# A two-block transformer kernel: expert up weights in two-row runs, expert rows turned by every second column, and a gather that leaves out empty slots

## The chip, the cores and the metric

One core of a Trainium2 chip runs the whole kernel. The metric is the device time of one launch in microseconds. All arithmetic is on float32 data. One profiled execution stands beside the timed runs. PE is the matrix engine (TensorE), PEld its weight loads, DVE, ACT and POOL are the vector, scalar and GpSimd engines, and SPq is the queue of the sync engine, which issues most DMAs.

## The reference, cut to what matters

The program is two transformer blocks over 512 tokens of 1024 features. Nearly all of it (the state-space, mLSTM and gated-linear-attention mixers, two convolutional feed-forward layers, sparse attention, memory attention) is the same before and after. The change is in the last part, a mixture of 32 experts of which each token takes two:

```
def hier_moe(h, w_rg, b_rg, w_re, b_re, w_up, w_down):
    g_logits = (h @ w_rg + b_rg)                      # 4 groups, one is taken
    e_logits = (h @ w_re + b_re)                      # 8 experts in a group, two are taken
    ...
    for n in range(N_EXPERTS):                        # 32
        a, b = jnp.split(h @ w_up[n], 2, axis=-1)     # w_up[n]: 1024 x 512
        out = out + combine[:, n:n + 1] * ((jax.nn.silu(a) * b) @ w_down[n])   # w_down[n]: 256 x 1024
    return out
```

`combine` is zero for every expert that a token did not take, so the kernel computes only the pairs of token and expert that count: 2 x 512 = 1024 of them.

## The kernel before

The expert part runs in four stages, each a block of instruction streams that all engines enter and leave together.

**Route** (line 3678) computes the two experts of each token on DVE. Meanwhile SP stores the normalised rows to a DRAM tensor (`normalised_rows`) and loads the weights of experts 0 and 1 ahead of need (`first_experts`, line 4258).

**Place** (line 3796) gives every pair of token and expert a slot. A block is 96 slots (`ROWS`) of one expert. Every expert has one block of its own, and there are ten more for experts with over 96 tokens (`NB` is 42). The result is `r.token`, the token number of each slot of each block, built by a product of 0/1 matrices on PE. A slot that nobody fills gets 0 from it, so the gather reads row 0 of the table for it. SP meanwhile writes zeros to the result rows of the ten further blocks. POOL has nothing to do in this stage.

**Experts** (line 3917) goes over the blocks. In the trace there are 32 of them, one per expert: 32 up loads, 32 down loads, 32 stores and 32 gathers. For block n the steps are:

- SP loads `up` (1024 x 512, 2 MB, into the buffer `ring`) and `down` (256 x 1024, 1 MB, into `moe_down`). Both have two sides, so a load goes to the side of the block two before. The up load of block n + 2 waits until the up products of block n are done (`up_done`). The down load of n + 1 waits until the down weights of n - 1 are split (`down_split`).
- POOL copies the 96 token numbers of the block and issues an indirect DMA (line 4010) that gathers 96 rows of 4 KB into one side of `e.rows` (`expert_rows`). It waits until the rows of block n - 2 have been turned.
- PE turns the gathered rows (`turn_rows`, line 4024): eight transposes of 96 x 128, each of them one weight load of the rows and one matmul against the identity. DVE copies the result to `e.x`.
- PE multiplies (`first`, line 4035): 32 products of a 128 x 128 piece of `up` with 96 columns of `e.x`, each two passes, so 64 matmuls in the trace.
- ACT and DVE apply silu and the gate, and split the hidden values and the down weights into a high and a low part (lines 4071 to 4139).
- PE multiplies by `down` (`second`, lines 384 to 386): 12 matmuls of 512 columns.
- ACT copies the result out of the accumulator and SP stores 96 rows to DRAM.

Each engine has a software pipeline written by hand: in step n, PE does `first(n + 1)`, then `turn_rows(n + 2)`, then `second(n)`. Two steps stand ahead of a loop, the loop takes two blocks a turn, and two steps stand behind it. SP's order in a step is down load of n + 1, up load of n + 2, store of n - 1.

The up weights are read by rows d = t * 128 + p, where p is the SBUF partition and t one of eight pieces. One partition so gets eight rows that lie 128 rows apart, as eight runs of 2 KB.

**Combine** (line 4158) gathers for each token its two result rows (eight indirect DMAs from POOL), scales and adds them on DVE, and stores the output.

Of the kernel before, what the change touches and what calls it, by code (L numbers as in the profile page):

```python
# [22 lines left out]
ALU = mybir.AluOpType  # L23
# [3 lines left out]
P = 128  # L27
T = 512
NT = T // P
# [37 lines left out]
NE, EPG, NG, EF = 32, 8, 4, 256  # L67
# [3722 lines left out]
ROWS = 96  # L3790
MOST = -(-T // ROWS)
NB = 2 * -(-(NE + SLOTS // ROWS) // 2)
FTE = EF // P


def place(k, r, zeros, y_dram, y_zeroed):

    nc = k.nc  # L3800
    with nc.Block(no_gpsimd_drain=True) as block:
        @block.sync
        def _(sp):
            sp.wait_ge(*k.sa(1))
            sp.dma_start(y_dram[NE * ROWS:, :].rearrange("(s p) d -> p s d", p=ROWS),
                         zeros[0:ROWS, :].rearrange("p (o d) -> p o d", o=1).to_broadcast([ROWS, NB - NE, D])).then_inc(y_zeroed, 16)
# [21 lines left out]
        def _(dve):  # L3828
            nc.vector.memset(zeros[:, :], 0.0).then_inc(k.sa.sem, 1)
            ps = k.ps[:, 0, :]  # L3830
# [43 lines left out]
            dve.drain()  # L3874
            nc.vector.tensor_copy(r.row[:, :], r.row_f[:, :])
            for t in range(NT):
                nc.vector.tensor_scalar(r.token_id[:, t:t + 1], ps[:, (NT + 1) * NE:(NT + 1) * NE + 1], float(t * P - 1), None, ALU.add)
            dve.drain()
            for n in range(2 * NT):
                nc.vector.tensor_scalar(r.is_slot[:, n, :], r.iota[:, 0:ROWS], r.rank[:, n:n + 1], None, ALU.is_equal)  # L3880
# [19 lines left out]
            nc.vector.tensor_scalar(r.before_last[:, :], r.count[:, :], -1.0, None, ALU.add)  # L3900
            nc.vector.tensor_scalar(r.expert[:, :], r.expert_f[:, :, 0], float(NE - 1), None, ALU.min)
            dve.wait_ge(*k.pb(1))
            nc.vector.tensor_copy(r.token[0:ROWS, :], k.ps[0:ROWS, 1, 0:NB])
    k.pa.close(1)
    k.va.close(1)
    k.pb.close(1)
# [3 lines left out]
def at_block(n, times=1, more=0):  # L3910

    if isinstance(n, tuple):
        return n[0] * (2 * times) + (n[1] * times + more)
    return n * times + more


def experts(k, r, rows_dram, y_dram, up, dn, e):
# [1 line left out]


    nc, A = k.nc, k.A
    wu = A["w_up_2"][0].rearrange("e (t p) n -> e p t n", p=P)
    wd = A["w_down_2"][0].rearrange("e (t p) n -> e p t n", p=P)

    XB, UB, YB = 0, 2, 4

    def side(n):
        return n[1] % 2 if isinstance(n, tuple) else n % 2

    def early(n, before):  # L3930

        return not isinstance(n, tuple) and n < before
# [5 lines left out]
    def pair_before_last(queue):  # L3938
        return queue.value_load(r.before_last[0:1, 0:1], min_val=0, max_val=NB // 2 - 2)
# [13 lines left out]
    def later(n, d):  # L3953

        return (n[0], n[1] + d, n[2]) if isinstance(n, tuple) else n + d

    def inside(n, d):

        return n[1] + d < n[2] if isinstance(n, tuple) else n + d >= 0

    with nc.Block(no_gpsimd_drain=True) as block:
        @block.sync
        def _(sp):
            def expert_of(n):
                at = at_block(n)
                one = r.expert[0:1, bass.ds(at, 1)] if isinstance(n, tuple) else r.expert[0:1, at:at + 1]
                return nc.sync.value_load(one, min_val=0, max_val=NE - 1)

            def load_up(n, expert):
                sp.dma_start(up[side(n)], wu[bass.ds(expert, 1)].rearrange("o p t n -> p (o t) n")).then_inc(e.up_loaded[side(n)], 16)  # L3970

            def load_down(n, expert):
                sp.dma_start(dn[side(n)], wd[bass.ds(expert, 1)].rearrange("o p t n -> p (o t) n")).then_inc(e.down_loaded[side(n)], 16)

            def of_last_pair(n):
                return isinstance(n, tuple) and n[1] >= 2 and n[2] == 4

            def store(n):
                sp.wait_ge(e.y_ready, at_block(n, 1, 1))
                sp.dma_start(y_dram[bass.ds(at_block(n, ROWS), ROWS), :] if isinstance(n, tuple) else y_dram[n * ROWS:(n + 1) * ROWS, :],  # L3980
                             e.y[0:ROWS, side(n), :]).then_inc(e.y_ended if of_last_pair(n) else e.y_stored[side(n)], 16)

            def step(n):
                if inside(n, -1) and inside(n, 1):
                    expert = expert_of(later(n, 1))
                    sp.wait_ge(e.down_split, at_block(n))
                    load_down(later(n, 1), expert)
                if inside(n, 2):
                    expert = expert_of(later(n, 2))
                    sp.wait_ge(e.up_done, at_block(n, 1, 1))  # L3990
                    load_up(later(n, 2), expert)
                if inside(n, -1):
                    store(later(n, -1))

            before = pair_before_last(nc.sync)
            sp.wait_ge(e.y_zeroed, 16)
            each_block(sp, before, step)
            store((before, 3, 4))

            sp.wait_ge(e.y_ended, 32)  # L4000

        @block.gpsimd
        def _(pool):
            def step(n):
                s = side(n)
                if not early(n, 2):
                    pool.wait_ge(e.turned, at_block(n, 1, -1))
                nc.gpsimd.tensor_copy(e.slot_token[0:ROWS, s:s + 1], r.token[0:ROWS, bass.ds(at_block(n), 1)] if isinstance(n, tuple) else r.token[0:ROWS, n:n + 1])
                pool.drain()
                nc.gpsimd.indirect_dma_start(e.rows[0:ROWS, s, :], None, rows_dram, bass.IndirectOffsetOnAxis(ap=e.slot_token[0:ROWS, s:s + 1], axis=0))\  # L4010
                    .then_inc(e.gathered[s], 16)

            each_block(pool, pair_before_last(nc.gpsimd), step)
            pool.drain()

        @block.tensor
        def _(pe):
            def turn_rows(n):
                s = side(n)
                pe.wait_ge(e.gathered[s], pair(n, 16))  # L4020
                if not early(n, 1):
                    pe.wait_ge(e.x_ready, at_block(n))
                for c in range(KD):
                    last = nc.tensor.transpose(k.ps[:, XB + c // NT, (c % NT) * ROWS:(c % NT + 1) * ROWS], e.rows[0:ROWS, s, c * P:(c + 1) * P], k.ident[0:ROWS, 0:ROWS])
                last.then_inc(e.turned, 1)

            def first(n):
# [177 lines left out]
def moe(k, out):  # L4205

    nc, A, sb = k.nc, k.A, k.alloc
    with ExitStack() as c:
        wr = router_place(k)
        r = Kernel()  # L4210
# [25 lines left out]
        e = Kernel()  # L4236
# [16 lines left out]
        up = [k.ring[:, s, :].rearrange("p (t n) -> p t n", t=KD) for s in range(2)]  # L4253
        dn = [down[:, s, :, :] for s in range(2)]
        rows_dram = nc.dram_tensor("normalised_rows", (T, D), F32, kind="Internal").ap()
        y_dram = nc.dram_tensor("expert_results", (NB * ROWS, D), F32, kind="Internal").ap()

        def first_experts(sp):
            for n in range(2):
                sp.dma_start(up[n], A["w_up_2"][0][n].rearrange("(t p) n -> p t n", p=P)).then_inc(e.up_loaded[n], 16)  # L4260
                sp.dma_start(dn[n], A["w_down_2"][0][n].rearrange("(t p) n -> p t n", p=P)).then_inc(e.down_loaded[n], 16)
        route(k, wr, r, k.ytmp[:, :, :], rows_dram, first_experts)
        place(k, r, e.zeros, y_dram, e.y_zeroed)
        experts(k, r, rows_dram, y_dram, up, dn, e)
        picked = k.ring[:, :, :].rearrange("p s n -> p (s n)").rearrange("p (n d) -> p n d", n=2 * NT)
        combine(k, r, y_dram, picked, out)
# [43 lines left out]
```

## Time and profile before

| | us |
|---|---|
| Median of 3 runs | 2733.13 |
| Lowest, highest | 2729.95, 2734.3 |
| Span of the profiled execution | 2731.6 |
| Mean granted TensorE clock | 0.973 |
| PE, PEld busy | 2544.9 (93%), 2032.0 (74%) |
| DVE, ACT, POOL busy | 1481.8 (54%), 1020.1 (37%), 226.4 (8%) |
| DMA | 329.04 MB, mean 120 GB/s |

The profiled execution's own time is its span, 2731.6 us from first to last instruction; the median of the runs is 1.5 us above that. The expert part is the last fifth: route begins at 2301 us, place at 2322, experts at 2345, combine at 2708. Shares of busy time over the whole span say little about it. The views have to be read for its own stretch, with the timeline of one block as the unit, since all 32 blocks do the same. A matmul's end in the trace is modelled, so the distance from one start to the next tells what it takes, and not its duration.

### The profile page before, as it was taken

To read this page: it belongs to the slowest core of one execution; us is meant where nothing else is said; L and a number is where in the kernel's file an instruction comes from. 1 tells how busy PE (TensorE), PEld (TensorE's weight loads), DVE (VectorE), ACT (ScalarE), POOL (GpSimd) and SP (SyncE) were. 2 spreads that over 40 slices of the span, in tenths; PEclk is the share of its full clock that TensorE was granted. 3 is DMA by queue.
4 is the path that set the end of the run, shared out by engine and by line. 5 is a ranking of instruction groups with operands and counts; after the bars stand their busy time and mean duration, and the time that the engine had idled before them with its cause. 6 is when DMAs were issued, how large, how long until landed. Compare 5 with 4: busy or idle time off the path is not lost. (4 is left out here: it accounts for less than half of the span.)

```text
span 2731.6 us, 34315 instructions
## 1 busy us (share of the span) xinstructions
PE 2544.9 (93%) x12689; PEld 2032.0 (74%) x12689; DVE 1481.8 (54%) x2251; ACT 1020.1 (37%) x1706; POOL 226.4 (8%) x260
## 2 busy tenths in 40 slices
PE   6999997789999999999999999999898988799995
PEld 5777786667888885766788887687586767699994
DVE  5766445654555534744555544477897564433333
ACT  3423342334544425423444433433334522133331
POOL 0000001000000000000000000555141000111111
PEclk9999999999999999999999999999999998799997
DMA  4122231032333321112333422222021013699995
GB/s 144 70 85 93 93 108 51 28 139 77 92 92 96 137 93 63 62 62 78 93 92 100 127 96 93 95 82 93 32 86 38 31 71 108 226 372 375 371 375 200
DMA packets 212513, 329.04 MB, mean 120 GB/s; under 512 B 13873, under 2 KB 110033, under 8 KB 212401
## 3 DMA queue, kind: packets, MB, share of 16 engines
q1 hardware_dynamic: 206784, 310.43, 33.1%
q0 software_dynamic: 4736, 16.78, 2.0%
q8 instruction: 70, 1.15, 0.2%
q10 hardware_dynamic: 881, 0.34, 0.0%
q14 instruction: 42, 0.34, 0.0%
HBM read 298.43 MB, written 29.10 MB: 120 GB/s over the span
## 5 line engine op out<-in xcount | busy, mean ns | idle before, releaser
L384 PE MATMUL ps<-ffn_parts 128*128 128x512 f32 x1056 | 411.6, 390 | 2.5 <-DVE ffn_parts L379 1.7
L386 PE MATMUL ps<-ffn_parts 128*128 128x512 f32 x1056 | 410.9, 389 | 0.0
L385 PE MATMUL ps<-ffn_parts 128*128 128x512 f32 x1056 | 410.8, 389 | 0.0
L4035 PEld LDWEIGHTS ps<-expert_x,ring 128*128 128x128 f32 x2048 | 235.0, 193 | 8.1 <-DVE expert_x L4119 3.3
L4035 PE MATMUL ps<-expert_x,ring 128*128 128x96 f32 x2048 | 234.9, 276 | 3.8 <-DVE expert_x L4119 3.0
L384 PEld LDWEIGHTS ps<-ffn_parts 128*128 128x128 f32 x1056 | 198.2, 188 | 46.5 <-issue 2.6
L386 PEld LDWEIGHTS ps<-ffn_parts 128*128 128x128 f32 x1056 | 198.2, 188 | 41.4
L385 PEld LDWEIGHTS ps<-ffn_parts 128*128 128x128 f32 x1056 | 198.2, 188 | 40.8
L379 DVE TENSOR_TENSOR ffn_parts<-ring,ffn_parts 128x1024 fp32r<-128x1024 f32 x132 | 157.7, 1223 | 117.9 <-ACT ffn_parts L2334 107.4
L379 POOL TENSOR_TENSOR w_lo<-ring,w_hi 128x512 fp32r<-128x512 f32 (+1 forms) x112 | 160.0, 1433 | 720.9 <-ACT w_hi L543 720.6
L2385 DVE SCALAR_TENSOR_TENSOR y_tmp<-ps,pcol,y_tmp 128x511 f32<-128x511 f32 x88 | 61.9, 745 | 214.0 <-ACT y_tmp L2318 214.0
L379 DVE TENSOR_TENSOR front_w_lo<-ring,front_w_hi 128x512 fp32r<-128x512 f32 x104 | 71.5, 688 | 138.6 <-ACT front_w_hi L925 138.4
L925 ACT CAST front_w_hi<-ring 128x512 fp32r<-128x512 f32 x104 | 63.9, 618 | 219.8 <-PE ps L386 219.7
L301 PE MATMUL ps<-brow,ident 128*128 128x512 f32 x238 | 119.1, 641 | 22.6 <-PEq L1827 6.1
L543 ACT CAST w_hi<-ring 128x512 fp32r<-128x512 f32 (+1 forms) x112 | 68.2, 610 | 185.4 <-PE ps L386 178.0
L379 DVE TENSOR_TENSOR expert_down_lo<-moe_down,expert_down_hi 128x1024 fp32r<-128x1024 f32 x64 | 75.5, 1222 | 96.4 <-ACT expert_down_hi L4079 96.4
L3331 DVE SCALAR_TENSOR_TENSOR conv_gate<-conv_u,pcol,conv_gate 128x512 f32<-128x512 f32 x120 | 114.2, 999 | 1.8
L384 PE MATMUL ps<-kept_hi,w_hi 128*128 128x512 f32 x256 | 101.5, 396 | 3.7 <-POOL w_lo L379 2.5
L2318 ACT ACTIVATE y_tmp<-ps,pcol 128x512 f32<-128x512 f32 x88 | 63.7, 774 | 109.7 <-PE ps L386 109.5
L384 PE MATMUL ps<-front_h_hi,front_w_hi 128*128 128x512 f32 (+1 forms) x232 | 97.5, 420 | 4.4 <-ACT hst L1256 2.7
L301 PEld LDWEIGHTS ps<-brow,ident 128*128 128x128 f32 x238 | 46.2, 205 | 74.5 <-issue 73.9
L384 PE MATMUL ps<-wo_hi,lhs_hi 128*128 128x512 f32 x256 | 100.5, 393 | 0.4 <-DVE lhs_lo L379 0.4
(636 smaller groups left out, 5210.1 us busy)
## 6 DMA issues: line engine op xcount, KB each, us to landing
ring<-in_w_up SPq DMA_DIRECT2D x32, 2048.0 KB, 11.4
ring<-in_ffn_w_up SPq DMA_DIRECT2D x88, 512.0 KB, 4.9
moe_down<-in_w_down SPq DMA_DIRECT2D x32, 1024.0 KB
ring<-in_ab_w_in SPq DMA_DIRECT2D x13, 2048.0 KB, 7.7
ring<-in_w_in SPq DMA_DIRECT2D x11, 2048.0 KB, 7.9
ring<-in_ffn_w_down SPq DMA_DIRECT2D x10, 2048.0 KB, 7.7
ring<-in_c_w_in SPq DMA_DIRECT2D x6, 2048.0 KB, 8.0
expert_results<-expert_y SPq DMA_DIRECT2D x32, 384.0 KB, 7.7
```

The source lines that it names most:

```text
L301: k.nc.tensor.matmul(k.ps[:, bank, :], k.ident[:, :], k.brow[:, 0:BANK], start=True, stop=True)
L379: return engine.tensor_tensor(lo, whole, hi.bitcast(F32), ALU.subtract)
L384: nc.tensor.matmul(out, left[0], right[0], start=start, stop=False, **more)
L385: nc.tensor.matmul(out, left[0], right[1], start=False, stop=False, **more)
L386: return nc.tensor.matmul(out, left[1], right[0], start=False, stop=stop, **more)
L543: nc.scalar.copy(part(w_hi, p), chunk(j)[:, rows, cols]).then_inc(k.w_hi_ready.sem, 1)
L925: k.nc.scalar.copy(self.part(0, p), self.raw(p)).then_inc(k.w_hi_ready.sem, 1)
L2318: last = nc.scalar.activation(ybuf[:, s, half, :], bank(s, half), ACT.Identity, bias=column(bias, i, s, half), scale=column(tap1, i, s, half))
L2385: nc.vector.scalar_tensor_tensor(out=ybuf[:, s, half, 1:T], in0=bank(s, half)[:, 0:T - 1], scalar=column(tap0, i, s, half), in1=ybuf[:, s, ...
L3331: nc.vector.scalar_tensor_tensor(out=y[:, j, :], in0=u[:, j, i:i + T], scalar=tap[:, n:n + 1], in1=y[:, j, :], op0=ALU.mult, op1=ALU.add)
L4035: last = nc.tensor.matmul(k.ps[:, UB + s, m * ROWS:(m + 1) * ROWS], up[s][:, c, m * P:(m + 1) * P], e.x[:, s, c, :], start=(c == 0), stop= ...
```

## The change

Four edits that belong together:

- `up_rows` and `up_runs` read and write the up weights so that a partition gets rows d = t * 256 + 2 * p and the one after it as one run of 4 KB, with t one of four pieces. The buffer, its size and the way `first` reads it stay: piece c now holds the rows t * 256 + 2 * p + b with t = c // 2 and b = c % 2.
- `turn_rows` has to turn the same features for piece c. It takes every second column of a stretch of 256 columns, beginning with column c % 2, where it took 128 columns in a row. There are still eight transposes of 96 x 128.
- `place` makes an unfilled slot's token number 1024 (2 * T) in place of 0: it subtracts 2 * T ahead of the product and adds it behind. The gather has a bounds check at row 511, and a number beyond it is skipped without an error.
- Rows that are skipped keep what was in the buffer. So that this is never uninitialised, `place` now clears `e.rows` on POOL (128 x 2048 values).

What is multiplied for filled slots is the same; what stands in unfilled slots is not read by combine.

```
+def up_rows(w):
+    return w.rearrange("e (t p b) n -> e p t (b n)", p=P, b=2)
+def up_runs(ap):
+    return ap.rearrange("p (t b) n -> p t (b n)", b=2)
...
-def place(k, r, zeros, y_dram, y_zeroed):
+def place(k, r, zeros, rows, y_dram, y_zeroed):
...
+        @block.gpsimd
+        def _(pool):
+            nc.gpsimd.memset(rows, 0.0)
+            pool.drain()
...
-                nc.vector.tensor_scalar(r.token_id[:, t:t + 1], ps[:, (NT + 1) * NE:(NT + 1) * NE + 1], float(t * P - 1), None, ALU.add)
+                nc.vector.tensor_scalar(r.token_id[:, t:t + 1], ps[:, (NT + 1) * NE:(NT + 1) * NE + 1], float(t * P - 1 - 2 * T), None, ALU.add)
...
-            nc.vector.tensor_copy(r.token[0:ROWS, :], k.ps[0:ROWS, 1, 0:NB])
+            nc.vector.tensor_scalar(r.token[0:ROWS, :], k.ps[0:ROWS, 1, 0:NB], float(2 * T), None, ALU.add)
...
-    wu = A["w_up_2"][0].rearrange("e (t p) n -> e p t n", p=P)
+    wu = up_rows(A["w_up_2"][0])
...
-                sp.dma_start(up[side(n)], wu[bass.ds(expert, 1)].rearrange("o p t n -> p (o t) n")).then_inc(e.up_loaded[side(n)], 16)
+                sp.dma_start(up_runs(up[side(n)]), wu[bass.ds(expert, 1)].rearrange("o p t n -> p (o t) n")).then_inc(e.up_loaded[side(n)], 16)
...
-                nc.gpsimd.indirect_dma_start(e.rows[0:ROWS, s, :], None, rows_dram, bass.IndirectOffsetOnAxis(ap=e.slot_token[0:ROWS, s:s + 1], axis=0))\
+                nc.gpsimd.indirect_dma_start(e.rows[0:ROWS, s, :], None, rows_dram, bass.IndirectOffsetOnAxis(ap=e.slot_token[0:ROWS, s:s + 1], axis=0), bounds_check=T - 1, oob_is_err=False)\
                     .then_inc(e.gathered[s], 16)
...
-                    last = nc.tensor.transpose(k.ps[:, XB + c // NT, (c % NT) * ROWS:(c % NT + 1) * ROWS], e.rows[0:ROWS, s, c * P:(c + 1) * P], k.ident[0:ROWS, 0:ROWS])
+                    features = e.rows[0:ROWS, s, (c // 2) * 2 * P:(c // 2 + 1) * 2 * P].rearrange("r (p b) -> r b p", b=2)[:, c % 2, :]
+                    last = nc.tensor.transpose(k.ps[:, XB + c // NT, (c % NT) * ROWS:(c % NT + 1) * ROWS], features, k.ident[0:ROWS, 0:ROWS])
...
-                sp.dma_start(up[n], A["w_up_2"][0][n].rearrange("(t p) n -> p t n", p=P)).then_inc(e.up_loaded[n], 16)
+                sp.dma_start(up_runs(up[n]), up_rows(A["w_up_2"][0])[n]).then_inc(e.up_loaded[n], 16)
```

PE, ACT, DVE and SP issue their instructions in the same order and number as before. On POOL one instruction comes in. From the end of route to the first two gathers its queue was, before:

```order
61 L3689 UNCONDITIONAL_BRANCH
62 L4002 UNCONDITIONAL_BRANCH
63 L3939 TENSOR_LOAD moe_before_last
64 L3939 ISA x2
65 L4008 COPY expert_slot_token<-moe_token 96x1
66 L4010 DMA expert_rows<-normalised_rows,expert_slot_token 96x1024
```

and it is, in the changed kernel (line 3954 there is line 3939 before, 4023 is 4008, 4025 is 4010):

```order
61 L3689 UNCONDITIONAL_BRANCH
62 L3812 UNCONDITIONAL_BRANCH
63 L3814 MEMSET expert_rows 128x2048
64 L3811 UNCONDITIONAL_BRANCH
65 L4017 UNCONDITIONAL_BRANCH
66 L3954 TENSOR_LOAD moe_before_last
67 L3954 ISA x2
68 L4023 COPY expert_slot_token<-moe_token 96x1
69 L4025 DMA expert_rows<-normalised_rows,expert_slot_token 96x1024
```

The memset stands in the place stage, where POOL had no instruction; everything behind it is in the old order.

## Rows read from the trace of the kernel before

**Rows 1.** The page: 40 slices of 68.3 us, busy tenths of PE, and GB/s
```profile
PE   6999997789999999999999999999898988799995
...
GB/s 144 70 85 93 93 108 51 28 139 77 92 92 96 137 93 63 62 62 78 93 92 100 127 96 93 95 82 93 32 86 38 31 71 108 226 372 375 371 375 200
```

**Rows 2.** Busy us of each engine by stretch; then clock, DMA share, GB/s
```profile
core 0: us, PE busy (x) PEld busy (x) DVE busy (x) ACT busy (x) POOL busy (x), PEclk, DMA share, GB/s
2400.00:2650.00 250.00, 250.00 (x1986) 230.29 (x1986) 94.89 (x144) 84.41 (x140) 26.81 (x48) 1.00 1.03 373
```

**Rows 3.** Timeline, weight loads, one block: start us, us, engine, line, operation, count
```profile
2480.80 7.34 PEld L4035 LDWEIGHTS ps<-expert_x,ring 128*128 128x128 f32 x64
2488.04 0.75 PEld L4024 LDWEIGHTS ps<-ident,expert_rows 96*128 96x128 f32 x8
2488.73 0.16 PEld L384 LDWEIGHTS ps<-expert_down_hi,expert_hid_hi 128*96 128x96 f32 x1
...
2491.37 7.34 PEld L4035 LDWEIGHTS ps<-expert_x,ring 128*128 128x128 f32 x64
...
2501.94 7.34 PEld L4035 LDWEIGHTS ps<-expert_x,ring 128*128 128x128 f32 x64
```

**Rows 4.** Waits of the matmul engine, 2345 to 2710 us: us in total, times, longest
```profile
PE ps L384 <- DVE expert_down_lo L379: 4.6, 1, 4.6
PE ps L4035 <- DVE expert_x L4119: 3.0, 2, 1.9
...
PE ps L4024 <- DMA expert_rows<-normalised_rows,expert_slot_token: 0.6, 1, 0.6
```

**Rows 5.** Line 3970, the up load, on the SP queue: 30 issues and their landing
```profile
L3970 SPq DMA_DIRECT2D ring<-in_w_up x30: 372/373/397, 2360.7 to 2668.1; - x30
...
DMA to landing us min/median/max: 9.0/11.3/12.7
```

**Rows 6.** Timeline of the SP queue in the block of Rows 3
```profile
2485.89 0.38 SPq L3973 DMA_DIRECT2D moe_down<-in_w_down  x1
2488.49 0.37 SPq L3970 DMA_DIRECT2D ring<-in_w_up  x1
```

**Rows 7.** The page's DMA queues, and loads by kind: KB each, us to landing
```profile
q0 software_dynamic: 4736, 16.78, 2.0%
...
ring<-in_ab_w_in SPq DMA_DIRECT2D x13, 2048.0 KB, 7.7
...
ring<-in_ffn_w_down SPq DMA_DIRECT2D x10, 2048.0 KB, 7.7
```

**Rows 8.** DMA view of 2296 to 2350 us, slices of 1.35 us
```profile
GB/s 0 0 0 0 231 370 400 352 206 231 338 370 364 422 423 402 401 394 388 411 428 382 346 334 282 291 337 325 285 240 106 55 30 0 0 0 0 0 0 249
```

**Rows 9.** Timeline of the matmul engine at the start of the expert stage
```profile
2345.18 5.46 PE L301 MATMUL ps<-brow,ident 128*128 128x512 f32 x6 [0.61 <-PEq L3801]
2351.18 0.88 PE L4024 MATMUL ps<-ident,expert_rows 96*128 96x96 f32 x8 [0.55 <-DMA expert_rows<-normalised_rows,expert_slot_token]
...
2353.18 7.22 PEld L4035 LDWEIGHTS ps<-expert_x,ring 128*128 128x128 f32 x64 [1.30 <-DVE expert_x L4119]
```

**Rows 10.** Windows of the same place, columns as in Rows 2
```profile
2346.00:2350.00 4.00, 4.00 (x6) 1.33 (x4) 0.00 (x0) 2.42 (x3) 1.47 (x3) 0.50 0.24 84
2350.00:2354.00 4.00, 2.33 (x16) 1.52 (x16) 1.90 (x3) 0.00 (x0) 1.13 (x2) 0.85 0.15 31
```

**Rows 11.** Line 4010, the gather: duration ns least, median, greatest; landing
```profile
L4010 POOL DMA_INDIRECT expert_rows<-normalised_rows,expert_slot_token x32: 937/938/1128, 2347.1 to 2659.2; - x32
...
DMA to landing us min/median/max: 3.9/7.5/8.7
```

**Rows 12.** Line 2566, a POOL memset of 128 by 2048
```profile
L2566 POOL MEMSET gla_att<- x1: 1806/1806/1806, 1126.4 to 1126.4; 128x2048 f32 x1
```

**Rows 13.** Timeline of DVE in the placement stage
```profile
2323.57 0.23 DVE L3835 TENSOR_SCALAR moe_iota<-moe_iota 128x128 f32<-128x128 f32 x1
2328.63 0.19 DVE L3838 TENSOR_SCALAR moe_blocks<-ps 128x32 f32<-128x32 f32 x1 [4.83 <-PE ps L3819]
```

More of the change, by code:

```diff
@@ L4259, in first_experts @@
             for n in range(2):
-                sp.dma_start(up[n], A["w_up_2"][0][n].rearrange("(t p) n -> p t n", p=P)).then_inc(e.up_loaded[n], 16)
+                sp.dma_start(up_runs(up[n]), up_rows(A["w_up_2"][0])[n]).then_inc(e.up_loaded[n], 16)
                 sp.dma_start(dn[n], A["w_down_2"][0][n].rearrange("(t p) n -> p t n", p=P)).then_inc(e.down_loaded[n], 16)
         route(k, wr, r, k.ytmp[:, :, :], rows_dram, first_experts)
-        place(k, r, e.zeros, y_dram, e.y_zeroed)
+        place(k, r, e.zeros, e.rows[:, :, :], y_dram, e.y_zeroed)
         experts(k, r, rows_dram, y_dram, up, dn, e)
```

## Prediction

> **What bounds the kernel now.** I began with the page's 40 slices [rows 1]: the traffic jumps from about 100 to 371-375 GB/s in slices 36 to 39, the expert stage, and nowhere else. That invites the reading "bound by DMA", and the change cuts traffic and packets there. But the same slices show PE at 9, so I asked the table by stretch [rows 2]: from 2400 to 2650 us PE is busy 250.00 of 250.00 us and PEld 230.29, with DMA at a share of 1.03 and 373 GB/s. Both look full, so busy shares don't decide it. What does is who waits for whom.
>
> The timeline of one block [rows 3]: 64 up passes start at 2480.80, the eight transposes at 2488.04, the 12 down products at 2488.73, the next up passes at 2491.37. So a block is 7.24 + 0.69 + 2.64 = 10.57 us, and the next one (2501.94) again 10.57. In the whole expert stage the waits of PE are few [rows 4]: 4.6 us at the end for the last down weights, which are split only behind the last copies, 3.0 us in two waits for the first columns, and 0.6 us for the first gather. None is for a weight load, and the first two are for DVE's work, not for bytes.
>
> Is PE itself slowed by the traffic? The first block's 64 up passes, with DMA at a share of 0.15 to 0.31, took 7.22 us [rows 9, 10]; under full traffic the same 64 take 7.24 from first start to the transposes. So no. And DMA keeps ahead: the up load of block n + 2 is issued at 2488.49 [rows 6] and is needed when the up passes after next begin, 2501.94 [rows 3], 13.45 us later. It lands after 11.3 us as a median and 12.7 at most [rows 5]. The least reserve is 13.45 - 12.7 = 0.75 us. It is thin, but it is there 30 times of 30. The loop is paced by PE. The DMA is busy because each block asks for 2048 + 1024 + 384 + 384 KB = 3.93 MB, and 3.93 MB / 10.57 us = 372 GB/s is the demand, not a ceiling: in the burst of route's stores and loads the queues moved up to 428 GB/s [rows 8].
>
> **The change part by part.** The sum is made against the span of 2731.6; the median of the runs lies 1.5 above it.
>
> (a) Up loads in 4 KB runs: 512 packets of 4 KB for 1024 of 2 KB. Two kinds of 2 MB load in this trace differ in just that: columns of `ab_w_in` come in 2 KB runs, rows of `ffn_w_down` in 4 KB runs, and both land after 7.7 us [rows 7]. So for a lone load I put the gain at 0. Among other transfers it may be above 0 or slightly below; either way it changes the reserve of 0.75 us, not the 10.57. It counts only if a load became over 6% slower (0.75 / 12.7), which the equal 7.7 excludes. 0 us.
>
> (b) Gather without empty slots: 32 x 96 = 3072 rows become 1024, so 2048 x 4 KB = 8.4 MB less, 0.26 MB a block, 6.7% of its 3.93 MB. In steady state a gather is issued just behind the turning of block n - 2 and used two periods later; it lands after 7.5 us, at most 8.7 [rows 11], of about 20. Cover: PE's own 21.1 us of work. 0 us. Exposed is the first gather alone: PE stands 0.55 us for it [rows 9]. If fewer rows land sooner, 0 to 0.55 us are won, beyond which the three filling products (to 2350.64) end last. If the check makes the descriptors' computation longer, it is lost; the nearest row is the least landing of a gather, 3.9 us, and one that took twice as long would cost 3.9. I take a gain of 0.3, since fewer rows mean fewer packets and the check is one comparison per row; ends -0.55 and +3.9.
>
> (c) The transposes read every second column. This is the one edit on the pacing engine: 8 x 32 = 256 weight loads, eight of them from 2488.04 to 2488.73, 86 ns each [rows 3]. No weight load of the trace has a stride of two. Bounds: no cost, since the 128 columns and 96 rows are the same; upward, reading at half the pace. A 128-column piece at the pace of the 512-column products (12 in 2.64 us, so 220 ns for 512 columns, 0.43 ns a column) is 55 ns, and twice that adds 55 ns x 256 = 14.1 us; all of a transpose doubled, 0.69 x 32 = 22.1 us. Below nothing is excluded: nothing is read less. I take 0, as the nearest row is the transpose itself, with the same columns, rows and count. This is a choice, not a reading, and the largest risk.
>
> On this the Trainium skill, Advanced Engine Details and Errata, section SBUF Cachelines, says that SBUF is read in lines of 16 bytes and that two hits on a line are enough for full pace. Four float32 values lie in a line, and every second one is two hits, so by that page the cost is 0; no row here shows it. Were the page wrong here, the sum would be the 14.1 us above.
>
> (d) The memset of 128 x 2048 on POOL: the trace has one of that very size, 1.81 us [rows 12]. It runs in place, where POOL has nothing else from 2322 to 2345. Even if it held up DVE's first instructions, DVE then idles 4.83 us for PE [rows 13], which covers 1.81; should the cover go, the cost is 1.81 at most. 0 us.
>
> (e) The two changed DVE instructions (another constant; an add for a copy, 96 x 42) are one for one: 0 us. PE's, SP's and ACT's instructions keep number and order.
>
> (f) The loads ahead in route: the traffic is at 0 by 2342 [rows 8], and the first up passes start at 2353.18. 0 us. The tail behind 2682 waits for ACT and DVE, and combine's eight gathers are untouched. 0 us.
>
> Sum: -0.3 us. 2731.6 - 0.3 = 2731.3, and with the 1.5 to the median 2732.8.
>
> **The rivals.**
>
> *Every second column costs (slower).* If a weight load at stride two is read at half pace, PE's block grows from 10.57 by 8 x 55 ns = 0.44 us and the whole by 14.1: 2733.1 + 14.1 = 2747.2. It speaks for it that PE has no gap to hide a nanosecond in; against it, that a transpose of 128 columns stands at 86 ns from the next where 128 columns at the pace of (c) are 55, so part of a slower load could lie in what is there already. From 5.5 us / 256 = 21 ns per transpose on it would show. Chance 0.10.
>
> *DMA sets the pace after all (faster).* If the 373 GB/s were the ceiling and PE only happened to look full (its ends are modelled), the block would shrink with its bytes: 0.26 MB / 373 GB/s = 0.70 us a block, over 31 blocks 21.8 us: 2711.3. For: DMA share 1.03, reserve 0.75 us. Against: no wait of PE for a load [rows 4], equal pace in light traffic [rows 9, 10], 428 GB/s seen [rows 8]. Chance 0.05.
>
> The Trainium skill speaks for this rival: DMA: Bandwidth & Descriptors, section "Where 436 GB/s comes from", has the HBM side bind at about 358 GB/s for a core. By that rule 373 would be past the ceiling and the stage bound by it. The trace disagrees: 373 is held for 250 us and 400 to 428 in a burst.
>
> *The checked gather is slow at the start (slower).* If the first gather takes twice its 3.9 us, PE stands 3.9 more, and its clock, 0.50 from 2346 to 2350 and 0.85 in the next four [rows 10], rises as much later; up to 4 us of work at half pace cost 2 more. 2733.1 + 5.9 = 2739.0. Chance 0.04. Later gathers have 21.1 - 8.7 = 12.4 us of reserve and don't matter.
>
> *The change doesn't do what it says.* Skipped rows may be moved anyway, or the packets stay at 2 KB. Then nothing is won, and by (a) and (b) nothing was to be won, so the time is as forecast. It lies within that case and is told apart by counts alone.
>
> **How the numbers follow.** A measurement of this kernel can tell about 0.2%, 5.5 us, from no change. Forecast within it: 0.80, at 2732.8. Faster: the DMA rival's 0.05 and 0.01 for something unseen, 0.06. Slower: 0.10 + 0.04 = 0.14. Same: 0.80. The range for 8 in 10: downward 0.55 for the gather, 3.2 for the spread of the runs (2733.13 to 2729.95) and two more for the median of other runs, 2727; upward it takes in the slow first gather, 2739.0, and 1 us for the spread, 2740. The cases at 2747 and 2711 stay out, 0.15 together, and 0.05 of the rest.
>
> **What would show it.** Right: the block still 10.57 us; PE 250.00 of 250.00 in mid-stage; the eight transposes still 0.69; GB/s in slices 36 to 39 down from 373 to about 348 (3.67 MB / 10.57); the software queue at 4736 - 2048 = 2688 packets and 8.4 MB, from the 4736 and 16.78 MB of before [rows 7]; up loads landing sooner than 11.3; the first wait of PE for the gather gone. Wrong: transposes longer than 0.69 (stride); a shorter distance between up passes (DMA or something in the passes); first transposes of the stage later than 2351.2 (gather); DVE's instruction at 2328.6 later (memset).

## The result, and the profile after

| | us |
|---|---|
| Changed kernel, median of 12 runs | 2739.59 (2735.72 to 2746.19) |
| Kernel before, median of 12 runs beside them | 2730.56 (2725.44 to 2738.81) |
| Ratio, 95% interval | 1.0033 (1.0021 to 1.0045) |
| Span of the profiled execution | 2737.8 |

The change costs 0.33%, 9.0 us of 2730.56. I had forecast 2732.8 and no change; 2739.59 lies just inside my range, but the sign was wrong: it is slower beyond its interval. That it lies inside is luck, as the part on the prediction says.

First the table by stretch for mid-stage, as [rows 2] has it of before, and the stage's start, as [rows 10]. The columns are busy us of PE, PEld, DVE, ACT and POOL, then granted clock, DMA share, GB/s.

```profile
2346.00:2350.00 4.00, 2.20 (x13) 1.94 (x13) 1.98 (x3) 0.00 (x0) 1.18 (x2) 0.89 0.10 22
2350.00:2354.00 4.00, 4.00 (x21) 4.00 (x21) 1.31 (x2) 0.00 (x0) 0.98 (x1) 0.50 0.11 28
2400.00:2650.00 250.00, 250.00 (x1940) 231.13 (x1940) 92.86 (x140) 83.74 (x138) 26.69 (x46) 1.00 0.93 338
```

PE is full in mid-stage, before and after. But in 250 us it gets 1940 matmuls done where it did 1986. DMA went from a share of 1.03 to 0.93, and 373 to 338 GB/s. So the traffic fell as meant, and the engine that it was not meant for became slower. The timeline of the weight loads shows where, against [rows 3]:

```profile
2482.98 7.35 PEld L4051 LDWEIGHTS ps<-expert_x,ring 128*128 128x128 f32 x64
2490.22 1.05 PEld L4040 LDWEIGHTS ps<-ident,expert_rows 96*128 96x128 f32 x8
2491.16 0.20 PEld L384 LDWEIGHTS ps<-expert_down_hi,expert_hid_hi 128*96 128x96 f32 x1
...
2493.82 7.35 PEld L4051 LDWEIGHTS ps<-expert_x,ring 128*128 128x128 f32 x64
```

The 64 up passes take 7.24 us, as before. The eight transposes take 0.94 for 0.69, the 12 down products 2.66 for 2.64. A block is 10.84 us for 10.57: 0.27 us more, 31 times over 8.4 us. The answer by line shows the weight load of a single transpose (least, median, greatest duration in ns), before and now:

```profile
L4024 PEld LDWEIGHTS ps<-ident,expert_rows x256: 138/140/171, 2351.2 to 2678.8; 96*128 96x128 f32 x128
...
L4040 PEld LDWEIGHTS ps<-ident,expert_rows x256: 195/216/218, 2346.8 to 2686.2; 96*128 96x128 f32 x128
```

A load is 76 ns longer. Loads overlap with their neighbours (140 ns long, 86 ns apart before), so what a transpose costs more is the distance from one start to the next: 0.25 / 8 = 31 ns.

The counts. The page's totals of before and of after, one from each:

```profile
DMA packets 212513, 329.04 MB, mean 120 GB/s; under 512 B 13873, under 2 KB 110033, under 8 KB 212401
```

```profile
DMA packets 196129, 320.66 MB, mean 117 GB/s; under 512 B 15921, under 2 KB 112081, under 8 KB 196017
q0 software_dynamic: 4736, 8.40, 1.0%
...
ring<-in_w_up SPq DMA_DIRECT2D x32, 2048.0 KB, 10.3
```

There are 16,384 packets fewer (32 loads times 512) and 8.38 MB less. The software queue has 8.40 MB for 16.78, but its 4736 packets are all there: 2048 more are under 512 B. A skipped row still sends a packet, with nothing in it. Up loads land after 10.3 us (11.4 on the page of before). The waits of PE in the stage are those of [rows 4] (the columns: line, what it waited for, us in total, times, longest):

```profile
PE ps L384 <- DVE expert_down_lo L379: 4.6, 1, 4.6
PE ps L4051 <- DVE expert_x L4135: 2.7, 2, 1.6
PE ps L4040 <- DMA expert_rows<-normalised_rows,expert_slot_token: 0.7, 1, 0.7
```

**The account of the profiled execution.** Its span grew by 6.2 us, which is not 8.4, so other things moved. The timeline at the start of the stage, against [rows 9]:

```profile
2340.93 5.18 PE L301 MATMUL ps<-brow,ident 128*128 128x512 f32 x6 [0.61 <-PEq L3811]
2346.79 1.20 PE L4040 MATMUL ps<-ident,expert_rows 96*128 96x96 f32 x8 [0.68 <-DMA expert_rows<-normalised_rows,expert_slot_token]
2349.10 10.47 PEld L4051 LDWEIGHTS ps<-expert_x,ring 128*128 128x128 f32 x64 [1.28 <-DVE expert_x L4135]
```

The stage began at 2340.93 for 2345.18, 4.25 us earlier. Of the change only the first two loads, the memset and two DVE instructions lie ahead of it, and neither part alone gives a gain in the medians below, so I don't count it as won. From there to the first gather of combine (2708.42 before, 2714.46 now) it took 373.53 us for 363.24, 10.29 more. By pieces between starts of up passes: 0.17 to the first; 3.52 from the first to the third, of which 3.25 is the first block's 64 passes alone, 10.47 us for 7.22; 7.71 from the third to the last; and 1.11 less behind the last. The sum is 10.29. The 3.25 is the clock, but not because it rose late. Asked by single microseconds, it rose here between 2345 and 2346, stood at 1.00 from 2346 to 2349, and was back at 0.50 from 2350 to 2355, under the first up passes (the 0.89 and 0.50 above). Before, it rose between 2351 and 2352 and stayed at 1.00 until 2364, so that the first block ran whole at 2.4 GHz. What PE did ahead of it is alike in both traces: six matmuls, a wait for the gather, eight transposes, a wait of 1.1 us for the columns. The 1.11 is the clock too: the last six down products, which started 0.43 us apart before, started 0.23 to 0.29 us apart now. Only the 7.71 is the block's 0.27. Whether the 3.25 belongs to the change is asked of the runs below.

### The profile page after: what moved, and what is told of

Read it like the earlier page. It is cut to its first block and busy times, and to the rows that moved or that the text cites. A ratio compares the mean times of both kernels' runs of the same rounds, so it can differ in the third digit from the quotient of the medians.

```text
span 2737.8 us, 34349 instructions
## 1 busy us (share of the span) xinstructions
PE 2552.6 (93%) x12689; PEld 2040.2 (75%) x12689; DVE 1482.0 (54%) x2251; ACT 1020.1 (37%) x1706; POOL 229.3 (8%) x261
## 2 busy tenths in 40 slices
DMA packets 196129, 320.66 MB, mean 117 GB/s; under 512 B 15921, under 2 KB 112081, under 8 KB 196017
## 3 DMA queue, kind: packets, MB, share of 16 engines
q0 software_dynamic: 4736, 8.40, 1.0%
## 6 DMA issues: line engine op xcount, KB each, us to landing
ring<-in_w_up SPq DMA_DIRECT2D x32, 2048.0 KB, 10.3
```

## The experiments

All ratios are against runs of the kernel before on the same chip. The first four divide the change into its parts.

### Only the columns

```
-  transpose(..., e.rows[0:ROWS, s, c * P:(c + 1) * P], ...)
+  features = e.rows[0:ROWS, s, (c // 2) * 2 * P:(c // 2 + 1) * 2 * P].rearrange("r (p b) -> r b p", b=2)[:, c % 2, :]
+  transpose(..., features, ...)
```

> The kernel before with one edit: the eight transposes of a block take every second column. Up weights stay in 2 KB runs, all 96 rows are gathered. Features and weight rows are paired wrongly, the work is the same. Theory (the weight load at stride two costs): the block grows from 10.57 to 10.84 us as in the changed kernel, the transposes from 0.69 to 0.94 and the step to the down products by 0.02, so 31 x 0.27 = 8.4 us, ratio about 1.0031. Rival (the loss comes with the gather's check or the first blocks' clock): ratio 1.000, block 10.57.

Measured: 2740.83 us for 2730.38; ratio 1.0033 (1.0022 to 1.0044). The timeline of one block, weight loads:

```profile
2475.65 7.35 PEld L4036 LDWEIGHTS ps<-expert_x,ring 128*128 128x128 f32 x64
2482.89 1.05 PEld L4025 LDWEIGHTS ps<-ident,expert_rows 96*128 96x128 f32 x8
...
2486.49 7.35 PEld L4036 LDWEIGHTS ps<-expert_x,ring 128*128 128x128 f32 x64
```

The block is 10.84 us. This one line alone gives the whole ratio of the change, with the traffic of before.

### Only the 4 KB runs

```
-  wu = A["w_up_2"][0].rearrange("e (t p) n -> e p t n", p=P)
+  wu = up_rows(A["w_up_2"][0])
-  sp.dma_start(up[side(n)], ...
+  sp.dma_start(up_runs(up[side(n)]), ...
```

> The kernel before with one edit: up weights in 4 KB runs. Transposes in plain columns, so features and weight rows are paired wrongly; the work is the same. Theory: block 10.57, ratio 1.000 +- 0.001; up loads land sooner than 11.3 us or equal, and nobody waits for them. Rival (fewer packets free the DMA and it sets the pace in part): ratio below 0.998.

Measured: 2730.36 us; 1.0002 (0.9992 to 1.0013). The block is 10.57 us (2474.07 to the next at 2484.63), the up loads land after 11.4 us as before, with 196129 packets for 212513. The edit is worth nothing here.

### Only the skipped rows

```
-  float(t * P - 1)             +  float(t * P - 1 - 2 * T)
-  tensor_copy(r.token, ...)    +  tensor_scalar(r.token, ..., float(2 * T), None, ALU.add)
+  nc.gpsimd.memset(rows, 0.0)
-  indirect_dma_start(...)      +  indirect_dma_start(..., bounds_check=T - 1, oob_is_err=False)
```

> The kernel before with one edit: empty slots skipped by the bounds check, with the memset. Computes the reference. Theory: block 10.57, ratio 1.000 +- 0.001, 338 GB/s in mid-stage, software queue 8.4 MB and still 4736 packets. Rival (the checked gather costs at the start and leaves the clock low in the first block, 10.47 us for its 64 passes against 7.22): ratio 1.0015, first up passes over 10 us.

Measured: 2729.64 us; 0.9993 (0.9983 to 1.0003). Its mid-stage traffic and the stage's first up passes:

```profile
2400.00:2650.00 250.00, 250.00 (x1986) 230.25 (x1986) 93.81 (x142) 85.28 (x142) 27.89 (x48) 1.00 0.99 347
```

```profile
2348.65 10.47 PEld L4040 LDWEIGHTS ps<-expert_x,ring 128*128 128x128 f32 x64 [1.30 <-DVE expert_x L4124]
2359.02 0.75 PEld L4029 LDWEIGHTS ps<-ident,expert_rows 96*128 96x128 f32 x8
```

PE does the same 1986 matmuls in 250 us, on 347 GB/s in place of 373 (the 338 that I had expected belongs to the longer block of the whole change). The edit is free and worth nothing. This kernel also has the 10.47 us in its first block, with plain transposes and a median that is not above that of before. So the 3.25 us can't be put down to the stride, and the medians show no such cost for the skipped rows: the same 64 passes took 7.22 us in the trace of before, 8.85 in those of the 4 KB runs and of the ordered rows (next), 10.39 with only the columns. One trace's start of the stage can be off by 3 us for the clock alone. That the stride makes the long first block likelier isn't excluded, since all three traces with strided transposes have it (every fourth column, below, too) and of five with the plain up and transpose loads only this one. The runs speak against it: the mean granted clock is 0.9749 over the 12 of the changed kernel and 0.9745 over the 32 of the kernel before.

### The whole change, rows put in order by ACT

The transposes are plain again. The columns are put in the order that the up weights now want when the rows go to DRAM, once for 512 rows:

```
-  transpose(..., features, ...)
+  transpose(..., e.rows[0:ROWS, s, c * P:(c + 1) * P], ...)
+  for t in range(NT):
+      nc.scalar.copy(ordered[:, t, :].rearrange("p (q b c) -> p q b c", b=2, c=P), rows[:, t, :].rearrange("p (q c b) -> p q b c", b=2, c=P))
+  sp.wait_ge(rows_ordered, 1)
-  sp.dma_start(rows_dram..., rows)     +  sp.dma_start(rows_dram..., ordered)
```

> The changed kernel, but the transposes take 128 columns in a row again. The order that the 4 KB runs need is made once, by ACT: in route it copies the four tiles of normalised rows (every second column first) into a buffer of its own, and SP stores that one for the gathers. Computes the reference. Theory: the stride moves from PE's 256 weight loads to four ACT copies of about 1.04 us that nobody waits for; block 10.57, ratio to before 1.000 +- 0.001. Rival: a stage behind the later store or the later prefetch starts late, ratio up to 1.0016 (4.5 us).

Measured: 2733.05 us; 1.0007 (0.9996 to 1.0018). A block, and the four copies on ACT:

```profile
2472.29 7.34 PEld L4054 LDWEIGHTS ps<-expert_x,ring 128*128 128x128 f32 x64
2479.53 0.75 PEld L4043 LDWEIGHTS ps<-ident,expert_rows 96*128 96x128 f32 x8
...
2482.86 7.34 PEld L4054 LDWEIGHTS ps<-expert_x,ring 128*128 128x128 f32 x64
```

```profile
2306.07 4.18 ACT L3775 COPY rows_ordered_sb<-y_tmp 128x1024 f32<-128x1024 f32 x4 [1.28 <-PEq L620]
```

The block is 10.57 again. Both DMA edits are in, all of the loss is out, and there is no gain. It is the better form of the change, not a better kernel than before. Whether the stride is free for ACT isn't settled by this: its four copies are 1.12 us long each and start 1.02 us apart, where its plain casts of a tile of that size (line 2313 before) are 1.05 us long and, two in a row, start 0.94 us apart. But a cast is another operation, and the difference is 0.08 us a copy at most, four times in all.

### Does the price grow with the stride?

My theory behind the first runs was that the load reads lines of SBUF and pays for the ones it touches: every fourth column touches twice as many as every second. The rival was a fixed price for a load that is not plain. Runs of four rows (8 KB) need every fourth column:

```
-  "e (t p b) n -> e p t (b n)", p=P, b=2    +  ... b=4
-  (c // 2) * 2 * P ... b=2)[:, c % 2, :]    +  (c // 4) * 4 * P ... b=4)[:, c % 4, :]
```

> The changed kernel with runs of four rows (8 KB) and transposes of every fourth column. Computes the reference. Theory (the price goes with the lines of 16 bytes that a weight load touches: 32 for 128 plain columns, 64 at stride two, 128 at stride four): going from stride one to two cost 32 ns a transpose, so two to four costs about 64 to 110 more, the block 11.3 to 11.7 us, ratio to before 1.008 to 1.013. Rival (any stride costs the same fixed 32 ns): block 10.84, ratio 1.0033. The Trainium skill, Advanced Engine Details and Errata, section SBUF Cachelines, has two hits on a line free and one hit slow: the measured stride two was not free.

Measured: 2741.01 us for 2729.78; 1.0033 (1.0021 to 1.0045). The answer by line, weight loads of the transposes:

```profile
L4040 PEld LDWEIGHTS ps<-ident,expert_rows x256: 197/219/222, 2348.9 to 2688.3; 96*128 96x128 f32 x128
```

The block is 10.84 again, the load 219 ns for 216. My theory asked for 11.3 to 11.7 and falls: stride four costs what stride two does.

### Every second value of the other operand

```
-  e.x[:, s, c, :]
+  e.x[:, s, c // 2 * 2:c // 2 * 2 + 2, :].rearrange("p a m -> p (a m)").rearrange("p (m b) -> p b m", b=2)[:, c % 2, :]
```

> The kernel before; the 64 up passes of a block read their moving operand (96 columns of expert_x) at every second column, the weights plain. Pairs features wrongly, the work is the same. Theory (a matmul's 96 columns hide beside the next weight load of 128, so a slower read of them has some cover): block 10.57 to 10.7, ratio below 1.002. Rival (the moving side pays 32 / 128 x 96 = 24 ns a pass uncovered): block longer by 1.5 us, ratio 1.018.

Measured: 2732.07 us; 1.0001 (0.9989 to 1.0012), block 10.56 us (up passes at 2454.21 and 2464.76). As the moving operand of all 2048 up passes, every second value is free. So the price belongs to the weights.

### What a pass waits for: columns or weights

The up passes multiply 64 of the 96 slots; the last 32 slots of each block are left out:

```
-  k.ps[:, UB + s, m * ROWS:(m + 1) * ROWS], ..., e.x[:, s, c, :]
+  k.ps[:, UB + s, m * ROWS:m * ROWS + 64],  ..., e.x[:, s, c, 0:64]
```

> The kernel before; the 64 up passes of a block multiply 64 columns in place of 96, the last 32 slots of a block are left out there. It asks how much of the 7.24 us goes with columns and how much with the 128-column weight loads, and whether PE time saved comes back as time. Theory: passes go from 113 to about 100 ns (route's passes of 36 columns were 182 ns apart at half clock, 91 at full), 0.8 us a block on PE, of which the DMA, paced at about 10 us a block in the half kernels, gives back only 0.6: ratio 0.993. Rival (weight loads alone set a pass): ratio 1.000.

Measured: 2746.39 us; 1.0053 (1.0034 to 1.0072), with a third fewer columns. Two places of its timeline:

```profile
2355.41 13.73 PEld L4035 LDWEIGHTS ps<-expert_x,ring 128*128 128x128 f32 x64 [1.30 <-DVE expert_x L4119]
2368.91 1.40 PEld L4024 LDWEIGHTS ps<-ident,expert_rows 96*128 96x128 f32 x8
2371.85 13.73 PEld L4035 LDWEIGHTS ps<-expert_x,ring 128*128 128x128 f32 x64 [1.54 <-DVE expert_x L4119]
...
2453.79 7.35 PEld L4035 LDWEIGHTS ps<-expert_x,ring 128*128 128x128 f32 x64
2461.00 0.75 PEld L4024 LDWEIGHTS ps<-ident,expert_rows 96*128 96x128 f32 x8
2464.32 7.35 PEld L4035 LDWEIGHTS ps<-expert_x,ring 128*128 128x128 f32 x64
```

In mid-stage a block is 10.53 us for 10.57, so a pass stays at 113 ns (7.21 / 64) with 64 columns for 96. It is paced by its weight load of 128 by 128, not by its columns, and my 100 ns was wrong. I had taken it from route's passes of 36 columns (line 3710), which I read as 91 ns apart at the full clock. They are 64 passes in 11.67 us with the clock falling among them: the first stand 112 ns apart at 1.00 and the others 213 at 0.50. The trace of before thus had the answer.

The loss is at the two ends of the stage. The traced run took 2754.45 us, the slowest of the five. In it the first two blocks ran whole at 1.2 GHz (granted clock 0.50 from 2356 to 2380) and took 35.18 us from the first up passes to the third, where before they took 21.96: 13.2 us. From the last up passes to the first gather of combine it took 32.0 us for 25.6, again at 0.50 for most of it. The low clock is not that one run's: the mean granted clock of the five is 0.965 to 0.970, of the 20 runs of before beside them 0.971 to 0.977. What PE did that delayed its clock is not settled.

### A strided load in an ordinary pass

The weights of the up products, every second hidden column, so that the hidden values come out in another order:

```
-  up[s][:, c, m * P:(m + 1) * P]
+  up[s][:, c, m // 2 * 2 * P:(m // 2 + 1) * 2 * P].rearrange("p (n b) -> p b n", b=2)[:, m % 2, :]
```

> The kernel before; the 64 up passes of a block load their 128 columns of weights at every second column (of 256), transposes plain. It permutes the hidden columns, the work is the same. Theory (a plain transpose loads its weights in a faster way, 86 ns apart, and a stride takes it back to about the pace of an ordinary float32 pass, 113 ns; so an ordinary pass has nothing to lose): block 10.57 to 10.8, ratio 1.000 to 1.002. Rival (any 128-column load at a stride pays 31 ns): block longer by 64 x 31 ns = 2.0 us, 62 us in all, ratio 1.023.

Measured: 2744.81 us for 2730.63; 1.0055 (1.0033 to 1.0077). Weight loads of a block:

```profile
2450.65 7.73 PEld L4035 LDWEIGHTS ps<-expert_x,ring 128*128 128x128 f32 x64
2458.27 0.76 PEld L4024 LDWEIGHTS ps<-ident,expert_rows 96*128 96x128 f32 x8
...
2461.60 7.73 PEld L4035 LDWEIGHTS ps<-expert_x,ring 128*128 128x128 f32 x64
```

The 64 passes take 7.62 us, 119 ns each, for 113. A block is 10.95 us for 10.57, which over 31 blocks is 11.8 us, a ratio of 1.0043. That lies inside the interval and above the 1.002 that my theory allowed, so an ordinary pass does have something to lose, if far less than the rival's 31 ns. A strided transpose takes 0.94 / 8 = 118 ns by the group, and 119 from one start to the next inside it. So both kinds end at the same 119 ns. A plain up pass stands at 113 ns and loses 6; a plain transpose stands at 86 ns and loses 32. That is what my terms had wrong: I asked how fast columns stream, and the question was how fast the load is, which is not the same for the two kinds.

Why a plain transpose stands at 86 can be read further in the trace of before, where other stages transpose too (weight loads by line; the last numbers before the waits are us busy and mean ns of one):

```profile
L4035 PEld LDWEIGHTS ps<-expert_x,ring 128*128 128x128 f32 x2048 | 235.0, 193 | 8.1 <-DVE expert_x L4119 3.3 <-issue 1.3
L662 PEld LDWEIGHTS ps<-ident,y_tmp 128*128 128x128 f32 x64 | 7.0, 140 | 6.1 <-DVE y_tmp L738 5.7
```

The transposes of line 662 have 128 rows and 128 moving columns. Their load is as long as that of the experts' transposes, 140 ns, but they stand 7.0 / 64 = 109 ns apart. With 96 columns it is 86. So a plain transpose goes with its columns (0.85 and 0.90 ns a column) and its load, shorter than the 193 ns of an ordinary pass, hides beside them, while the ordinary pass and every strided one go with the load. From this an estimate: a stride in a transpose of 128 columns would cost 119 - 109 = 10 ns, not 32. No run tried it, and the two kinds of transpose differ in their rows as well.

### What the DMA edits are worth when PE is out of the way

Half of the up products are left out (`for c in range(0, KD, 2)`), in four kernels: of before, with the 4 KB runs, with the skipped rows, and with both (rows ordered as above). PE then needs 10.57 less 3.62, 6.95 us a block.

> The kernel before with half of the up products left out (every second piece c), so that PE needs 3.62 + 0.69 + 2.64 = 6.95 us a block and no longer sets the pace; loads, gathers and stores are all there. Theory: the 3.93 MB a block now take at least 3.93 / 428 = 9.2 us, so the block lands at 9.2 to 9.8 us and PE waits for up loads. If the DMA had been the pace before too, the block would stay at 10.57 and the time at ratio 1.000.

> As h1_half_before, with the up weights in 4 KB runs. Where DMA sets the pace this tells what fewer packets are worth. Theory (packets cost little, since lone loads of both kinds land after 7.7 us): block as in h1_half_before to 0.1 us. Rival (a packet costs a fixed time): block shorter by up to 0.5 us, 15 us in all.

> As h1_half_before, with the empty slots skipped. Theory: 6.7% fewer bytes, block shorter by 0.26 MB / 400 GB/s = 0.6 us, 20 us in all (ratio to h1_half_before about 0.993).

> As h1_half_before, with 4 KB runs, skipped slots and the rows put in order by ACT in route, so without the stride on PE. Theory: the sum of the two before it, block about 0.6 to 0.8 us shorter than h1_half_before, nothing lost to the stride.

| up products halved | median us | ratio to before (interval) | us a block, issues | us a block, mid-stage |
|---|---|---|---|---|
| nothing else | 2714.40 | 0.9934 (0.9915 to 0.9954) | 10.24 | 10.34 |
| 4 KB runs | 2709.62 | 0.9910 (0.9893 to 0.9926) | 10.04 | 10.17 |
| skipped rows | 2700.07 | 0.9880 (0.9863 to 0.9897) | 9.78 | 9.92 |
| both | 2698.98 | 0.9874 (0.9857 to 0.9890) | 9.60 | 9.72 |

The fourth column is from the first to the last of the 30 up issues, over 29. It takes in the first blocks, whose loads were done ahead; for the kernel before it is 10.60. The last column is from the fifth up passes to the thirtieth (2386.16 and 2644.70 in the first kernel), over 25, and it is the one to hold against 10.57. Three answers of the first kernel: by stretch, PE's waits from 2380 to 2620 us, and the up loads:

```profile
2400.00:2600.00 200.00, 152.65 (x1011) 129.69 (x1010) 78.39 (x119) 69.85 (x117) 22.34 (x40) 0.94 1.04 378
```

```profile
PE ps L4035 <- issue: 31.7, 12, 3.5
PE ps L4035 <- DMA ring<-in_w_up: 24.0, 11, 3.2
```

```profile
L3970 SPq DMA_DIRECT2D ring<-in_w_up x30: 372/373/397, 2354.9 to 2651.9; - x30
...
DMA to landing us min/median/max: 11.2/15.6/17.0
```

Taking 3.62 us of PE's work out of every block gave back 0.23 in mid-stage; I had expected 9.2 to 9.8 us a block. PE now stands before its up passes once a block, 23 times in 240 us. For 11 of these waits (24.0 us) the trace names the up load, for 12 (31.7 us) it names nothing. The load lands after 15.6 us where it took 11.3 [rows 5]. A block's 3.93 MB in 10.34 us are 380 GB/s, and the table has 378 at a DMA share of 1.04. So the DMA sets the pace here, and in the kernel before it was 0.23 us a block from doing so, no more. How much of this is the rate of the transfers and how much that a load waits for its buffer, these runs don't separate.

In this setting the skipped rows are worth 14.3 us (2714.40 to 2700.07), with intervals that do not touch, and 0.42 us a block, where I had expected 0.6. The 4 KB runs are worth 4.8 us with intervals that overlap, and both together are not measurably better than the skipped rows alone. The traces lean towards a small gain of the 4 KB runs: 0.17 us a block without and 0.20 with the skipped rows, one trace each, between my theory (0.1 at most) and its rival (0.5).

The blocks of mid-stage are not the whole of the 18 us that the ratio 0.9934 gives. In the first kernel's trace the stage, up to the first gather of combine, is 345.6 us for 363.2. Of these 17.6 us the 25 blocks give 5.6, the four before them 4.7, and what lies behind the thirtieth up passes 7.5.

## Why the prediction was wrong, point by point

**What bounds the kernel: right, by less than I made of it.** PE paces the loop. The block of the two DMA edits alone and of both together stays 10.57 us. But I took 373 GB/s for a demand far from any ceiling because a burst of stores and loads had shown 428 [rows 8]. With PE out of the way the stage sustains 373 to 384 GB/s. The reserve that I read as 0.75 us on one load was, per block, 0.23 us. The burst was mostly the weight loads of the first two experts, for some 14 us (ten slices of 1.35), without the gathers and result stores of the stage, and was no evidence for it.

**(a) 4 KB runs, 0 us: right.** 1.0002, landing unchanged at 11.4 us with only this edit.

**(b) Skipped rows, -0.3: wrong in the reason and in a count.** 0.9993 can't be told from nothing, so the size is neither confirmed nor refuted. The least landing is 3.6 us for 3.9, the instruction on POOL takes 982 ns for 938 [rows 11], and PE stood 0.68 us for it, not 0 to 0.55 less. The queue kept its 4736 packets; I had 2688.

**(c) Every second column, 0 us: the step that failed.** It costs 0.25 us in the eight transposes and 0.02 behind them, 8.4 us over the stage: the median's 9.0. My bounds, 0 and 14.1, held it; my choice between them did not. I took 0 because "the nearest row is the transpose itself", which compared an operation with itself under the one condition that had changed. The trace had a nearer row that I did not use: in [rows 3] eight transposes take 0.69 us, 86 ns each, and 64 up passes 7.24, 113 ns each, both loading 128 columns of float32. So a transpose's load ran faster than an ordinary one and had something to lose. A bound of 113 - 86 = 27 ns times 256 would have given 6.9 us; measured were 31 to 32 ns and 8.4. Even this would have been a little low, since a strided load is slower than an ordinary one too (119 ns).

My rule of half pace gave 55 ns and 14.1 us, too much. The Trainium skill, Advanced Engine Details and Errata, section SBUF Cachelines, has two hits on a line of 16 bytes as enough, and gave 0. The runs disagree at both ends: stride two costs 31 ns where that rule has none, and stride four, with one hit a line, costs no more (219 ns a load for 216).

**(d), (e), (f), 0 us: right.** The memset took 1.81 us at 2317.8 and nothing came later for it. From the first gather of combine to the end it is 23.3 us for 23.2.

**The rivals.** "Every second column costs" happened, with 31 ns for 55; I gave it 0.10. "DMA sets the pace" is false here, since taking bytes away moved no block; it becomes true 0.23 us further on. There the rule that I weighed against the trace (the Trainium skill, DMA: Bandwidth & Descriptors, section "Where 436 GB/s comes from", 358 GB/s on the HBM side for a core) is nearer than my 428: 373 to 384 were sustained. "The checked gather is slow at the start" did not happen: 3.6 us. A first block 3.25 us longer in the profiled execution looks like it and isn't, as the kernel with only the skipped rows has it too at no cost of its median.

**The range.** 2739.59 is below its end of 2740 by luck. That end was set by the slow first gather, which did not happen; the case that did happen I had at 2747.2 and outside.

**The chances.** 0.80 for no change was too much for a sum whose one term on the pacing engine I had called "a choice, not a reading, and the largest risk". An unseen form of an instruction on the engine that paces, 256 times, with 21 ns enough to show, deserved more than 0.10.

What stays open: what makes the plain transpose's load faster than an ordinary float32 load (140 ns long for 193), whether pairs or longer runs of columns would keep it, and what decides when the clock rises and falls in the first two blocks. No run here settles these.

## What to carry to other kernels

Find the engine that paces the loop, and price every edit on it first, however small, before the edits that the change is about. A new access pattern on that engine is an unknown, and its first bound is the slowest other form of the same instruction in the trace, not the form that it replaces. Leave room above it: here that form stood at 113 ns and the new one came out at 119. If data must be reordered, do it once on an engine with room (four copies on ACT, 4.18 us beside other work) and not in each block on PE. And before traffic is cut for speed, ask how far the DMA is from setting the pace: here it was 0.23 us of 10.57 short of it, and fewer bytes bought nothing.

## What the runs showed of the hardware

- A float32 weight load with a stride in its 128 columns puts passes 119 ns apart. For a transpose of 96 columns (86 ns plain) it makes no difference whether the stride is two or four; an ordinary product (113 ns plain) was tried at two.
- The moving operand may have a stride of two at no cost (block 10.56 us for 10.57).
- A plain float32 transpose stands 86 ns from the next with 96 moving columns and 109 with 128 (line 662 before), with a load of 140 ns in both.
- A float32 pass with 128 by 128 weights takes 113 ns for 96 columns and for 64, and 112 for 36 (route, line 3710).
- A row that an indirect DMA skips by its bounds check saves its bytes but not its packet (4736 before and after), and makes the issuing instruction 44 ns longer (982 for 938).
- The same 64 up passes at the start of the stage took from 7.22 to 10.47 us in traces of kernels that leave them as they are, and 13.73 with 64 columns, for the clock alone. A single trace can't price an edit there.
